# Opening in quarters of the first weight block, the function table loaded early, and constant products in four waits of TensorE

## What is computed

```
for layer in range(DEPTH):
    h = rmsnorm(x, attn_norm[layer])
    m = diff_attention(h, da_w_qkv[slot], ...)   # layer 0: s = q k^T * scale + bias, softmax, values
    x = x + m @ w_o[layer]
    ...
```

## Time and profile before

| | us |
|---|---|
| median of 3 runs | 1784.57 |
| the runs | 1783.97 to 1784.65 |
| the profiled execution | 1784.35 |
| its span in the profile | 1782.6 |
| PE busy in the span | 1763.1 (99%) |
| DVE, ACT, POOL busy | 1249.8, 1001.0, 82.2 |

### The profile page before, as it was taken

One profiled execution on the slowest core, in us unless ns is written; L12 is line 12 of the kernel. 1 busy time (PEld: TensorE's weight loads), 2 busy tenths in 40 slices (PEclk: granted clock), 3 DMA queues, 4 the chain that ended last, 5 costly groups with the idle time before them and its releaser, 6 DMA issues.

```text
span 1782.6 us, 35585 instructions
## 1 busy us (share of the span) xinstructions
PE 1763.1 (99%) x14304; PEld 1719.1 (96%) x14304; DVE 1249.8 (70%) x1811; ACT 1001.0 (56%) x1494; POOL 82.2 (5%) x138
## 2 busy tenths in 40 slices
PE   8999999999999999999999999999999999999998
PEld 7999999999999998999999999999999999999997
DVE  7667868766787886787876687798555776565555
ACT  5676555655655566655566755566443655355343
POOL 2000000011000013000000000003000020000000
PEclk9999999999999999999999999999999999999999
DMA  9445655543565545565554456556555544436552
GB/s 298 151 143 159 198 187 161 182 139 122 166 203 182 168 168 166 166 202 182 167 191 139 147 175 204 181 176 199 187 181 178 167 165 140 167 111 204 180 179 93
DMA packets 238423, 306.34 MB, mean 172 GB/s; under 512 B 13698, under 2 KB 212916, under 8 KB 238268
## 3 DMA queue, kind: packets, MB, share of 16 engines
q1 hardware_dynamic: 236692, 300.27, 51.9%
q0 software_dynamic: 1504, 4.28, 0.7%
q10 hardware_dynamic: 104, 0.07, 0.0%
HBM read 303.53 MB, written 1.07 MB: 171 GB/s over the span
## 4 chain that ended last, share of the span: by engine, by line
PE 94%; ACT 3%; DVE 2%; issue 1%; DMA 0%; DVEq 0%; ACTq 0%
PE ps L1002 29%; PE ps L1003 29%; PE ps L1004 29%; PE ps L1167 1%; ACT sb_w_hi L831 1%; DVE sb_w_lo L1544 1%; PE ps L1187 0%; PE ps L1254 0%; PE ps L1217 0%; PE ps L1204 0%; PE ps L1159 0%; PE ps L1015 0%; PE ps L1281 0%; DMA sb_work<-in_x 0%; PE ps L1242 0%
## 5 line engine op out<-in xcount | busy, mean ns | idle before, releaser
L1002 PE MATMUL ps<-sb_a_hi,sb_w_hi 128*128 128x256 f32 x3120 | 894.0, 287 | 6.9 <-ACT sb_a_hi L878 3.1
L1003 PE MATMUL ps<-sb_a_lo,sb_w_hi 128*128 128x256 f32 x3120 | 884.3, 283 | 0.0
L1004 PE MATMUL ps<-sb_a_hi,sb_w_lo 128*128 128x256 f32 x3120 | 884.1, 283 | 0.0
L1544 DVE TENSOR_TENSOR sb_w_lo<-sb_raw,sb_w_hi 128x2048 fp32r<-128x2048 f32 x283 | 646.8, 2291 | 328.8 <-ACT sb_w_hi L831 328.5
L831 ACT ACTIVATE sb_w_hi<-sb_raw 128x2048 fp32r<-128x2048 f32 x283 | 538.3, 1906 | 242.8 <-PE ps L1004 233.9
L1002 PEld LDWEIGHTS ps<-sb_a_hi,sb_w_hi 128*128 128x128 f32 x3120 | 599.7, 192 | 16.5 <-issue 10.1
L1003 PEld LDWEIGHTS ps<-sb_a_lo,sb_w_hi 128*128 128x128 f32 x3120 | 599.9, 192 | 0.8
L1004 PEld LDWEIGHTS ps<-sb_a_hi,sb_w_lo 128*128 128x128 f32 x3120 | 599.8, 192 | 0.0
L1002 PE MATMUL ps<-sb_hh,sb_w_hi 128*128 128x256 f32 x912 | 257.1, 282 | 0.0
L1003 PE MATMUL ps<-sb_hl,sb_w_hi 128*128 128x256 f32 x912 | 256.8, 282 | 0.0
L1004 PE MATMUL ps<-sb_hh,sb_w_lo 128*128 128x256 f32 x912 | 256.6, 281 | 0.0
(11 more groups left out here) (232 smaller groups left out, 1435.1 us busy)
## 6 DMA issues: line engine op xcount, KB each, us to landing
sb_raw<-in_ffn_w_up SPq DMA_DIRECT2D x102, 1024.0 KB, 5.4
sb_raw<-in_ffn_w_down SPq DMA_DIRECT2D x66, 1024.0 KB, 4.9
sb_raw<-in_da_w_qkv SPq DMA_DIRECT2D x24, 1024.0 KB, 6.4
sb_raw<-in_ffn_w_gate SPq DMA_DIRECT2D x22, 1024.0 KB, 5.3
sb_raw<-in_w_o SPq DMA_DIRECT2D x16, 1024.0 KB, 4.9
sb_raw<-in_sb_w_qkv SPq DMA_DIRECT2D x12, 1024.0 KB, 5.2
sb_raw<-in_xa_wkv SPq DMA_DIRECT2D x8, 1024.0 KB, 5.3
sb_raw<-in_w_in SPq DMA_DIRECT2D x8, 1024.0 KB, 5.6
```

The costliest lines, as they stand in the source:

```text
L1002: pe.matmul(o, hi1, hi2, start=start, stop=False, skip_group_check=True)
L1003: pe.matmul(o, hi1, lo2, start=False, stop=False, skip_group_check=True)
L1004: return pe.matmul(o, lo1, hi2, start=False, stop=stop, skip_group_check=True)
L1544: dve.tensor_tensor(w_lo[:, a % RING, :], raw[:, a % RING, :], w_hi[:, a % RING, :].bitcast(F32), ALU.subtract).then_inc(lo_ready, 1)
```

## The change

1. Block 0 is loaded in two DMAs of four chunks each; the first signals `s_half_block`, the second `raw_ready` as before.
2. ACT loads the set with exponential and logarithm as its first work. It makes the first half of block 0's hi in two quarters, behind two chunks of activations instead of four, and the second half behind six.
3. DVE copies two pairs of x, makes two lo chunks and the first quarter's lo, copies the third pair, makes the second quarter's lo and two lo chunks, copies the fourth pair, and goes on as before. The table's scaling (`s_tab`) moves behind the lo of block 1. PE waits for a quarter at k = 0 and at k = 2.
4. `keep_warm` multiplies a 128x128 matrix of ones by the identity into a bank that nobody reads: 3 times ahead of the norms' rows, 6 times ahead of x, 6 times behind the table's product, and 12 times behind the sum of squares at the bridge without blocks.

```diff
@@ block.sync, mixer blocks
+                        if ph["n"] + i == 0:
+                            sp.dma_start(slot(0, KC)[:, 0:4, :], src[:, 0:4, :]).then_inc(s_half_block, 16)
+                            load(0, 0, slot(0, KC)[:, 4:8, :], src[:, 4:8, :])
+                            continue
@@ block.scalar
+            exp_and_ln(act)
             act.wait_ge(s_gain, 1)
             prep_hi(phases[0], 0)
+            act.wait_ge(s_half_block, 16)
+            for i in range(2):
+                es = slice(i * BE // 4, (i + 1) * BE // 4)
+                act.activation(w_hi[:, 0, es], raw[:, 0, es], ACT.Copy).then_inc(first_hi, 1)
             prep_hi(phases[0], 1)
+            prep_hi(phases[0], 2)
             act.wait_ge(raw_ready[0], 16)
-            act.activation(w_hi[:, 0, 0:BE // 2], raw[:, 0, 0:BE // 2], ACT.Copy).then_inc(first_hi, 1)
             act.activation(w_hi[:, 0, BE // 2:], raw[:, 0, BE // 2:], ACT.Copy).then_inc(hi_ready, 1)
-            prep_hi(phases[0], 2)
             prep_hi(phases[0], 3)
@@ block.tensor
             def bridge(ph):
                 if not ph["blocks"]:
-                    return square_total_of_four(ph)
+                    square_total_of_four(ph)
+                    keep_warm((ph["u"] + 3) % 4, 12)
+                    return
@@
-                            if ph["n"] == 0 and k == 0:
-                                pe.wait_ge(first_lo, 1)
+                            if ph["n"] == 0 and k in (0, 2):
+                                pe.wait_ge(first_lo, k // 2 + 1)
@@
+            def keep_warm(bank, n):
+
+                for _ in range(n):
+                    pe.matmul(UB[bank][:, 0:P], ones[:, :], ident[:, :], start=True, stop=True, skip_group_check=True)
+
             pe.wait_ge(s_const, 2)
+            keep_warm(3, 3)
             pe.wait_ge(s_first, 16)
...
             ins.then_inc(s_setup_pe, 1)
+            keep_warm(3, 6)
             pe.wait_ge(s_xin, 16)
...
                 .then_inc(s_setup_pe, 1)
+            keep_warm(3, 6)
@@ block.vector
-            for i in range(4):
+            def take_x(i):
                 dve.wait_ge(s_setup_pe, i + 2)
                 dve.tensor_copy(x[:, 2 * i:2 * i + 2, :], pairs(DB[i])).then_inc(x_ready, 1)
+
+            def first_quarter(i):
+                es = slice(i * BE // 4, (i + 1) * BE // 4)
+                dve.wait_ge(first_hi, i + 1)
+                dve.tensor_tensor(w_lo[:, 0, es], raw[:, 0, es], w_hi[:, 0, es].bitcast(F32), ALU.subtract)\
+                    .then_inc(first_lo, 1)
+
+            take_x(0)
+            take_x(1)
             dve.wait_ge(s_gain, 1)
             lo_pair(phases[0], x, 0)
-            dve.wait_ge(first_hi, 1)
-            dve.tensor_tensor(w_lo[:, 0, 0:BE // 2], raw[:, 0, 0:BE // 2], w_hi[:, 0, 0:BE // 2].bitcast(F32), ALU.subtract)\
-                .then_inc(first_lo, 1)
+            first_quarter(0)
+            take_x(2)
+            first_quarter(1)
             lo_pair(phases[0], x, 1)
+            take_x(3)
             dve.wait_ge(hi_ready, 1)
...
             for i in (2, 3):
                 lo_pair(phases[0], x, i)
+            split(1)
             dve.wait_ge(s_setup_pe, 6)
             dve.tensor_scalar(table_sb, UB[1][0:16, 0:TW], ROOT_HD, None, ALU.mult).then_inc(s_tab, 1)
-            split(1)
             prep(phases[0])
```

More of the change, by code:

```diff
@@ L280, in model_kernel @@
         s_poolw = sem("s_poolw")
+        s_half_block = sem("s_half_block")
         first_hi = sem("first_hi")
```

## The result

The changed kernel takes 1791.32 us (median of 7 runs, 1789.75 to 1791.58) against 1784.65 (7 runs of the kernel before, beside it): a ratio of 1.0033, 95% interval 1.0023 to 1.0042. That is 5.9 us above the forecast of 1785.4 and above the end of the range, 1787.6. The profiled execution took 1789.75 with a span of 1788.0. It is one of three runs at 1789.75 to 1790.26; the other four are at 1791.32 to 1791.58. So the trace explains 5.4 us (1788.0 less the 1782.6 of before), and the median is 1.6 us above it.

A forecast was written before the change was run, and what follows sets the result against it. TensorE was taken as bound by ACT's chain in the opening, then by the bias load. The late bias cost 1.2 us, the transition gained 0.25: +0.95 on 1784.35, about 1785.4 us; range 1782.4 to 1787.6.

The forecast's parts named there:

- the two waits of before: TensorE's idle 2.9 us before the first weight block's first product and 3.1 us late; other waits would follow.
- block 1 hangs on ACT's chain: Opening: ACT's unbroken work sets block 1's start, so only 0.7 of the 1.28 us is left, 20.0 for 20.67.
- the moved table scaling: DVE scales the bias table behind block 1's lo, 3.3 us later; the scores lose 1.2 us.
- the late write: POOL's write of the scaled table, issued at 20.7, lands at 26.1 and releases the bias load near 26.4.
- the second scores: Second group of score matmuls: TensorE there at 38.7, waits about 2 us for the bias, starts 40.6 against 39.41.
- block 1's slow products: If the clock falls in the 2.7 us wait before block 1: one or two us, hidden by the next step.
- The transition: Late in the kernel: 12 constants keep the clock up, but the next block's lo limits the gain to 0.25 us.
- I take 10.8, the same load in the same place: The 2 MB bias load, issued near 26.4, keeps its 10.8 us; bounds 9.1 and 14.3.
- Rival 3: Late bias load meets block 6, takes 14.3 us; TensorE waits 3.5 us more, perhaps slower clock: 1788.9 us, chance 0.08.
- a us or so if the clock falls: Allowance in the range only, for a fall of the clock in the new wait.
- I take 0: Six constants ahead of the x transposes, 1.3 to 2.7 us in 2.13 idle: no net delay.
- The price of the table load: ACT's opening: loading the function table early takes 1.28 us out of its chain, with no drain counted.

The follow-up runs named there:

- experiment 1: Changed kernel with the table's scaling put back ahead of the lo of block 1: 1785.7 us, ratio to the kernel before 1.0008.
- experiment 2: Kernel before with only the table's scaling moved behind the lo of block 1: 1792.26 us, ratio 1.0040.
- experiment 6: Kernel before with only the 12 constants of the transition added: 1784.65 us, ratio 1.0000.
- experiment 8: Changed kernel with the bias loaded and masked in two parts, heads 0 to 3 first: 1785.45 us, ratio to the kernel before 1.0005.
- Experiment 5: Changed kernel with SP issuing block 5, and all behind it, only when the bias has landed: 1786.31 us, ratio to the kernel before 1.0012.
- experiment 7: Kernel before with only ACT's function table loaded early, as its first work: 1786.01 us, ratio 1.0010.
- experiment 3: Changed kernel without the 3, 6 and 6 constants of the opening: 1790.07 us, ratio to the kernel before 1.0026.
- experiment 4: Changed kernel with the table's scaling ahead of block 1's lo and ten constants ahead of block 1: 1785.87 us, ratio to the kernel before 1.0011.
- experiment 9: Changed kernel without the opening's constants, table scaled first, bias in two parts, ACT's hi of block 1 ahead of the squares: 1781.57 us, ratio to the kernel before 0.9980.

## Why the prediction was wrong

**Right.** The prediction had it right that the two waits of before would be followed by others, that block 1 hangs on ACT's chain, and that the moved table scaling is the part that costs. It had the path too: the late write (20.7 forecast, 21.28 measured), the load released by it, and the second scores as the place where it shows, with the engine that ends the wait. It was also right that block 1's slow products would hide beneath that wait. The transition was right to the size: 0.25 forecast, 0.27 measured, with the clock at 1.00 and 1.5 us of wait for the lo. Experiments 1 and 2 bear out the table scaling, experiment 6 the transition, experiment 8 the hidden products.

**Wrong, the size of the load.** The step that failed is "I take 10.8, the same load in the same place": it took 13.1 in the profiled run and 15.3 in experiment 2. With the issue 0.6 late on top (26.98 for 26.4, because the scaling began at 20.45 and not 19.9) the scores were 3.0 us later than forecast, 43.61 for 40.6. "In the same place" was the error. What counts is the load's place among the other loads. In the kernel before it was issued at 24.14, a us ahead of block 5's (25.17); in the changed kernel it is issued at 26.98, 1.4 us behind block 5's (25.54), and even the forecast 26.4 was behind. Experiment 5 shows that it is this rank and not the hour: as late, but with nothing ahead of it, the load took 9.2.

Rival 3 had this mechanism, with block 6 in block 5's part, 14.3 us, and 1788.9 as its time. It got a chance of 0.08, and the range stopped short of it. The row of block 6, a load that was issued behind others and took 14.3, was the nearest row for a load that comes second. Even so rival 3 lies 2.4 us below the median; it names the fall of the clock, but its time has no term for it.

**Wrong, the fall of the clock.** The forecast of 2 us of wait at the second scores went into the sum without the slow products behind it; "a us or so if the clock falls" stood in the range only. It was 1.5 us, and both waits of before had shown the same. It does not come each time: in experiments 1 and 7 the same wait, of 2.4 and 2.9 us, had no fall behind it. The two terms, 3.0 and 1.5, are the 4.5 us between the forecast for the profiled execution (1784.35 + 0.95 = 1785.3) and what it took. The median is another 1.6 above, and no trace of the changed kernel shows one of its slower runs. A longer load, as in experiment 2, would do it, but that was not seen. More time at half the clock is unlikely: the mean granted clock is 0.998, 0.998, 0.998 and 0.997 in the four slower runs and 0.997, 0.998 and 0.997 in the three faster ones, and 1.6 us of it would have lowered it by 0.001.

**Wrong, but without effect on the time.** "I take 0" for the constants ahead of x: they cost 1.0 us at x and 0.8 at block 1 (experiment 3), so that block 1 came 0.08 sooner and not 0.7. The three constants ahead of the norms' rows did not fit either (these began at 3.33, in the kernel before at 2.88), so the six began late, at 4.27, and their 12 records took 2.93 us where I put 2.7 at most. (The rows behind that price, hold two products of two records, not three; the 0.22 between them was read rightly.) In the changed kernel this lay beneath the wait for the bias. In experiment 4, where the bias is in time, nothing is left of the 1.28 us taken from ACT: block 1 starts at 20.84, against 20.67 in the kernel before. The price of the table load was right, nothing but its 1.28 went. "ScalarE: Activation LUTs", What ACT_TABLE_LOAD costs, of the Trainium skill has a drain behind it as well. The traces do not: in experiment 7, without the load, ACT's first chunk begins at 7.94, and before it began at 9.22, 1.28 apart to the hundredth.

## What to carry to other kernels

A load keeps its duration only if it keeps its rank among the loads. When an edit moves the issue of one transfer past another's, or another's past it, price it by the row of a load that came second. Look for a near tie in the kernel before, too: experiments 1 and 4 differ only in constants ahead of block 1, and the load came second in the trace of one and first in that of the other. A small instruction on the way to a DMA (here one of 0.54 us) belongs ahead of a large one that is merely next. Constants that keep the clock up pay only where nothing but TensorE's own pace stands behind them. A wait that is left costs itself and often the slow products after it; put both into the sum, unless a later wait hides them.

## What the runs showed of the hardware

- Where SP's and POOL's queues both move, they move packet for packet (75 and 75 in the kernel before from 29 to 30, 68 and 68 from 32 to 33), and the larger packet has the larger share: the bias, at 4 KB a packet, had about 80% of the engines there and the weights, at 1 KB, about 24%. But the load that comes second has nothing at first: in experiment 1 block 5's bytes moved from before 27 on and those of the bias, issued 0.2 us earlier, only after 29. Why it stays shut out for so long was not found.
- The 2 MB took 9.2 us with nothing else in flight, 10.8, 10.9 and 11.3 when first (the kernel before, experiments 6 and 4), 11.4 to 15.3 when second.
- With nothing else in flight POOL's load, issued at 27.12 (experiment 5), moved its first byte at 29.0, 1.9 us later; SP's block 5, issued at 36.34 when the bias had landed, moved its first at 37.3, 1.0 us later. That difference of 0.9 fits it that a lead of 0.2 us in the issue was lost and one of 1.0 us held.
- A wait of about one length has a fall of the clock behind it or not. Ahead of block 1, 2.4 us brought 0.50 (1.2 GHz) in each of the five traced runs that had it (the changed kernel, experiments 1, 3, 5 and 8), but the clocks of some runs without a trace speak against it there too. At the second scores 2.75 and 6.2 us did, and 1.3, 2.4 and 2.86 us did not. What decides was not found.
- The profile's clock reads 1.00 at the start although TensorE works at half pace there: in experiment 9 the first products of block 0 stand 0.21 us apart from 11.3 to 12, where the column says 1.00, and those of block 1 stand 0.12 apart. The 16 transposes of x took 3.38 to 3.68 us in the nine traces without constants ahead of them. Behind constants they took 2.13 to 2.58 us in four traces and 3.46 in the fifth (experiment 8), so the constants brought the full pace by then as a rule and not each time.
